# Dilated attention by pairs of heads: alternating row halves and banks for the scores, column halves for the weighing, one bias addition and one maximum per pair

## Chip, cores and metric

One core of a Trainium2 chip runs the kernel, written in Bass: every engine has its own program and waits on semaphores. The metric is device microseconds of one execution.

## What is computed

Two transformer blocks on one sequence of 256 tokens with 1024 channels, in float32: a first block with a recurrent branch, windowed attention and 32 experts, then two layers of feed-forward, mixer, feed-forward. The change is in the mixer of the last layer, dilated attention with 16 heads of 64 channels and three dilation groups. Cut to what matters:

```
qkv = (h @ w_qkv).reshape(B, T, N_GROUPS, 3, N_HEADS_2, HEAD_DIM)
for g, (window, dilation) in enumerate(DILATION_GROUPS):      # (128,1) (512,4) (2048,16)
    q = rmsnorm_2(qkv[:, :, g, 0], q_gain[g]) * (HEAD_DIM ** -0.5)
    k = rmsnorm_2(qkv[:, :, g, 1], k_gain[g])
    v = qkv[:, :, g, 2]
    logits = q k + bias, masked;  m = max;  p = exp(logits - m);  s = sum(p);  o = p v / s
    lse = m + log(s)
wts = softmax(stack(lses), axis=0)
o = sum over g of wts[g] * o[g];  return o @ w_out
```

The kernel does the three groups of a head as one softmax over their keys side by side, which is the same weighted sum.

## The kernel before

**Dense layers.** The weights come by DMA in float32 and are split into two parts whose sum is the weight: ScalarE (ACT) makes the high part (`hi_tile`, L317), VectorE (DVE) the low part (`lo_tile`, L321), TensorE (PE) multiplies with both. Layer `qkv` (72 tiles of 128 tokens by 256 columns) takes 8 chunks a tile, each one 512-column and one 256-column product (L379, L380). ACT and DVE then each take half of the result (L413, L420). Four tiles of split weights exist at a time.

**Turns.** The 16 heads are worked in four turns of four heads, each with 18 tiles of `qkv`: six with values, twelve with queries and keys. Those twelve are also squared (L1930), summed (L2109), rooted (L1918, the Sqrt table of ACT), normalised (L2104), turned on PE (L2016) and taken back (L1926). The attention of a turn is put between the chunks of the next turn's tiles. The last turn stands in the first three tiles of layer `attn_out` (L371, L372), whose chunks 6 and 7 need the last two output pairs.

**A unit of attention** is a head x and a query block b, eight units to a turn. Block 0 sees 128 keys in each group, block 1 sees 256. Its steps are: scores on PE (three products of 64 rows, L2027) into bank 3 and, for block 1, half of bank 4; on DVE the addition of the bias (L2121) and the negated maximum (L2124); Exp with its sum on ACT (L1936); on DVE reciprocal and scaling into EN (L2129, L2131); 3 or 6 transposes on PE (L2037) into bank 5, for block 1 also 6; the copy into ETX on ACT (L1945); the weighing on PE (3 or 6 products with 64 output rows, L2051) into bank 7, row half x % 2. When a pair of heads is done, ACT and DVE split its output (`out_high` L1957, `out_low` L2145), on which `attn_out` waits.

**Order.** Everything is in order of its engine's program. `STEP_BEFORE` puts ten steps 6 chunks apart from tile 4 on; step i holds the scores of unit i, the transposes of unit i-1 and the weighing of unit i-2. On ACT and DVE the steps of a turn stand among the work on a tile (`ahead`, `between`, `behind` of `run_layer`), so a step there cannot begin before the tile in front of it is out of PE. In float32 every product is two records of PE; a transpose is one.

## Time and profile before

| | |
|---|---|
| median of three runs | 2504.03 us (2503.38 to 2504.77) |
| the profiled execution, its time / its span | 2507.36 us / 2505.5 us |
| PE busy / DVE busy / ACT busy | 2397.6 us (96%) / 1404.2 us (56%) / 1010.7 us (40%) |
| `qkv` and its attention, up to the end of the last weighing | about 1960 us to 2291 us of the span |

Shares are of the whole span. The stretch of the change is about an eighth of it, and there DVE and ACT are much busier than on average, so it has to be read by windows. A PE row's duration includes its way through the array: how long PE is held is read from the distance of starts.

### The profile page before, as it was taken

How to read it: one execution, taken by the hardware profiler on the slowest of the kernel's cores; microseconds unless marked ns; L12 is line 12 of the kernel's file. 1: busy time of each engine (PE TensorE's matmuls, PEld its weight loads, DVE VectorE, ACT ScalarE, POOL GpSimd, SP SyncE). 2: the span in 40 equal slices, each digit the busy share in tenths (PEclk: the TensorE clock that was granted, in tenths of full speed). 3: DMA queues.
4: the chain of work that ended last, by engine and by line, in shares of the span. 5: the costliest groups of instructions: out<-in, count | busy, mean ns of one | idle time of the engine just before them, and what ended most of it. 6: DMA issues, size and time to landing. Idle time of an engine off the chain costs nothing.

```text
span 2505.5 us, 35586 instructions
## 1 busy us (share of the span) xinstructions
PE 2397.6 (96%) x13302; PEld 1655.2 (66%) x13303; DVE 1404.2 (56%) x2712; ACT 1010.7 (40%) x1858; POOL 75.7 (3%) x125
## 2 busy tenths in 40 slices
PE   6999999999999999999989999999999999998999
PEld 3777854444444444444468888888888778876888
DVE  5688742223222223222267779786786677776785
ACT  3645531111111111111155556654654566664653
POOL 0000000000000000000000000000000110001000
PEclk8999999999999999999999999999999999999999
DMA  8764679999999999999965555555555665552553
GB/s 311 246 230 141 215 322 424 425 426 425 425 425 425 426 426 425 426 426 425 424 223 185 180 178 182 186 184 187 183 182 193 178 137 137 141 137 71 172 181 122
DMA packets 277971, 673.68 MB, mean 269 GB/s; under 512 B 8484, under 2 KB 236111, under 8 KB 244960
## 3 DMA queue, kind: packets, MB, share of 16 engines
q1 hardware_dynamic: 274656, 663.60, 69.8%
q0 software_dynamic: 3200, 8.53, 2.5%
q8 instruction: 75, 1.23, 0.2%
q14 instruction: 40, 0.33, 0.0%
HBM read 670.45 MB, written 1.12 MB: 268 GB/s over the span
## 4 chain that ended last, share of the span: by engine, by line
PE 86%; DVE 7%; ACT 3%; DMA 2%; issue 2%; DVEq 0%; ACTq 0%; SPq 0%
PE PS L371 25%; PE PS L1454 17%; PE PS L372 13%; PE PS L1476 9%; PE PS L379 6%; PE PS L1441 5%; PE PS L380 3%; PE PS L1428 2%; DVE WS L321 2%; DMA RING<-in_moe_w 1%; PE PS L2027 1%; PE PS L2051 1%; DVE XG L1571 1%; DMA RAW<-in_w_ada 1%; PE PS L2037 1%
## 5 line engine op out<-in xcount | busy, mean ns | idle before, releaser
L371 PE MATMUL PS<-HN,WS 128*128 128x512 f32 x1952 | 704.1, 404 | 16.2 <-DVE WS L321 10.3
L321 DVE TENSOR_TENSOR WS<-RAW,WS 128x1024 fp32r<-128x1024 f32 (+1 forms) x452 | 541.0, 1205 | 136.9 <-ACT WS L317 131.3
L372 PE MATMUL PS<-HN,WS 128*128 128x256 f32 x1952 | 551.0, 282 | 0.0
L317 ACT ACTIVATE WS<-RAW 128x1024 fp32r<-128x1024 f32 (+1 forms) x452 | 463.2, 1034 | 85.8 <-PE PS L372 71.5
L1454 PE MATMUL PS<-RING,XG 128*64 128x512 f32 x2048 | 447.0, 594 | 12.0 <-DVE XG L1571 10.9
L371 PEld LDWEIGHTS PS<-HN,WS 128*128 128x128 f32 x1952 | 370.9, 190 | 111.3 <-DVE WS L321 12.5
L372 PEld LDWEIGHTS PS<-HN,WS 128*128 128x128 f32 x1952 | 373.0, 191 | 0.3
L1454 PEld LDWEIGHTS PS<-RING,XG 128*64 128x64 f32 x2048 | 148.8, 137 | 295.9 <-issue 292.3
L1577 DVE TENSOR_SCALAR GLU<-PS 128x256 f32<-128x256 f32 x64 | 27.2, 425 | 414.9 <-PE PS L1454 414.9
L371 PE MATMUL PS<-MI,WS 128*128 128x512 f32 x704 | 247.7, 397 | 0.0
L1476 PE MATMUL PS<-RING,AT 128*64 128x512 f32 x1024 | 226.8, 594 | 14.8 <-ACT AT L1350 14.8
L1343 ACT ACTIVATE SIG<-GLU 128x256 f32<-128x256 f32 x64 | 26.7, 417 | 520.6 <-DVE GLU L1577 520.6
L379 PE MATMUL PS<-WS,HN 128*128 128x512 f32 x576 | 215.1, 412 | 6.2 <-DVE WS L321 3.2
L372 PE MATMUL PS<-MI,WS 128*128 128x256 f32 x704 | 197.6, 281 | 0.0
L1476 PEld LDWEIGHTS PS<-RING,AT 128*64 128x64 f32 x1024 | 84.6, 137 | 136.4 <-issue 135.2
L380 PE MATMUL PS<-WS,HN 128*128 128x256 f32 x576 | 162.9, 283 | 0.0
L371 PEld LDWEIGHTS PS<-MI,WS 128*128 128x128 f32 x704 | 132.1, 188 | 32.0
L1571 DVE TENSOR_TENSOR XG<-PS,SH 128x512 f32<-128x512 f32 x32 | 22.1, 692 | 201.3 <-PE PS L1441 201.3
L1441 PEld LDWEIGHTS PS<-PSEL,H2K 128*128 128x128 f32 x1024 | 116.7, 192 | 25.9 <-issue 25.2
L372 PEld LDWEIGHTS PS<-MI,WS 128*128 128x128 f32 x704 | 133.0, 189 | 0.0
L379 PEld LDWEIGHTS PS<-WS,HN 128*128 128x128 f32 x576 | 109.5, 190 | 34.2 <-issue 4.1
L1441 PE MATMUL PS<-PSEL,H2K 128*128 128x64 f32 x1024 | 121.1, 276 | 0.3 <-DVE PGAT L1566 0.3
(356 smaller groups left out, 2635.4 us busy)
## 6 DMA issues: line engine op xcount, KB each, us to landing
RING<-in_moe_w SPq DMA_DIRECT2D x192, 2048.0 KB, 22.4
RAW<-in_ffn_w_in SPq DMA_DIRECT2D x88, 1024.0 KB, 5.2
...
```

Of the source, the lines that this page charges most:

```text
L317: act_f(split_tile(0, n), raw_tile(n), ACT.Copy).then_inc(hi_done, 1)
L321: vec.tensor_tensor(split_tile(1, n), raw_tile(n), split_tile(0, n).bitcast(f32), ALU.subtract).then_inc(lo_done, 1)
L371: nc.tensor.matmul(both, hi[:, k, :], x2[:, :, kx, :], start=start, stop=False)
L372: ins = nc.tensor.matmul(half, lo[:, k, :], x2[:, 0, kx, :], start=False, stop=stop)
L379: nc.tensor.matmul(both, x2[:, 0, kx, x], w2, start=start, stop=False)
L380: ins = nc.tensor.matmul(half, x2[:, 1, kx, x], w2[:, 0], start=False, stop=stop)
L1428: nc.tensor.matmul(bank[COMB[m]][:, :], PGT[64 * g:64 * g + 64, tt * P:(tt + 1) * P], YE[64 * g:64 * g + 64, :], start=True, stop=True).th ...
L1441: last = nc.tensor.matmul(bank[4][:, k * SLOTS:(k + 1) * SLOTS], H2K[:, tt, k * P:(k + 1) * P], PSEL[:, tt, :], start=tt == 0, stop=tt == ...
L1454: last = nc.tensor.matmul(bank[j][64 * side:64 * side + 64, :], XG[:, 2 * q + k, :], w[:, k, 1024 * side + 512 * j:1024 * side + 512 * (j ...
L1476: last = nc.tensor.matmul(bank[6][64 * side:64 * side + 64, :], AT[:, b, 64 * q:64 * q + 64], w[:, b, 512 * side:512 * (side + 1)], start= ...
L1571: TTN(XG[:, :, :], bank[4][:, :].rearrange("p (k s) -> p k s", k=DC), SH2[:, :].rearrange("p (k a) -> p k a", a=1).to_broadcast([P, DC, SL ...
L1577: TS(GLU[:, halves[j]], pairs[:, halves[j], 0], 7.0, None, ALU.min).then_inc(sem("clamped"), 1)
```

## The change

Two heads (x = 0 and 1, a pair p) are now one unit q, four to a turn; odd q are block 1.

- **Scores** (`scores`): head 0 uses rows 0 to 63 and bank 3, head 1 rows 64 to 127 and bank 4, one product of each in turn. For block 1 only two groups fit the banks; the third is a step of its own (`late_scores`), which waits until DVE has added the bias to the first two.
- **Weighing** (`weigh`): the products of the two heads alternate, writing partitions 0 to 63 and 64 to 127 of bank 7.
- **Bias and maximum** (`bias`): one addition over both heads and one maximum for two heads; for block 1 the addition is in two parts, 2x512 and 2x256 columns.
- **Exp, scaling, transposes, copy** remain one of each per head. For block 1 both heads' transposes use banks 5 and 6, so the odd head's wait until ACT has copied the even head's.
- **Places**: tables of offsets in chunks, units 12 chunks apart from chunk 28 on (tile 3, chunk 4). The last turn has a list for each engine.
- ES holds both heads, UB is one tensor, and the loads of a pair's bias wait for the pair.

```
-        ES = [rg(f"ES{i}", [N_GROUPS * S]) for i in range(2)]
+        ES = [rg("ES0", [2, N_GROUPS * S])]
...
+        ES.append(Region(rg.o)("ES1", [2, N_GROUPS * S]))
         DX = rg("DXT", [DC, S])
-        UB = [Region(ub0 + i * 3 * KB)(f"UB{i}", [N_GROUPS, S]) for i in range(4)]
+        UB = Region(ub0)("UB", [TURN, N_GROUPS, S])
...
-        STEP_BEFORE = {(4 + 6 * i // DC, 6 * i % DC): i for i in range(NU + 2)}
-        STEPS_AT = {w: [i for (v, k), i in STEP_BEFORE.items() if v == w + 1] for w in range(3, 10)}
-        LAST_BEFORE = {(1, 0): 0, (1, 3): 1, (2, 0): 2, (2, 3): 3}
-        OUT_AT = {11: 1}
...
-        def score_bank(n):
-            return PS[:, 3 * 512:3 * 512 + N_GROUPS * n]
-
-        def turn_bank(n):
-            return PS[:, 5 * 512:5 * 512 + N_GROUPS * n]
+        UNITS, ROUNDS = TURN, 3 * TURN // 2
+        BEGIN, APART = 28, 12
+        PE_STEPS = {"scores": 0, "late_scores": 5, "turn_even": 14, "turn_odd": 17, "weigh": 22}
+        DVE_STEPS = {"scale_even": 10, "scale_odd": 12, "bias": 0, "late_bias": 5, "out_low": 25}
+        ACT_STEPS = {"exp": 8, "take_even": 15, "take_odd": 18, "out_high": 24}
+        LAST_BEFORE = {(1, 1): [("scores", 0)], (1, 4): [("scores", 1)], (2, 1): [("late_scores", 1)], (2, 4): [("scores", 2)]}
+        LAST_PE = [("turn_even", 0), ("turn_odd", 0), ("scores", 3), ("weigh", 0), ("turn_even", 1), ("turn_odd", 1),
+                   ("late_scores", 3), ("weigh", 1), ("turn_even", 2), ("turn_odd", 2), ("weigh", 2),
+                   ("turn_even", 3), ("turn_odd", 3), ("weigh", 3)]
+        LAST_DVE = [("bias", 0), ("bias", 1), ("late_bias", 1), ("scale_even", 0), ("scale_odd", 0), ("bias", 2),
+                    ("scale_even", 1), ("scale_odd", 1), ("bias", 3), ("late_bias", 3), ("out_low", 1),
+                    ("scale_even", 2), ("scale_odd", 2), ("scale_even", 3), ("scale_odd", 3), ("out_low", 3)]
+        LAST_ACT = [("exp", 0), ("exp", 1), ("take_even", 0), ("take_odd", 0), ("exp", 2), ("take_even", 1), ("take_odd", 1),
+                    ("out_high", 1), ("exp", 3), ("take_even", 2), ("take_odd", 2), ("take_even", 3), ("take_odd", 3),
+                    ("out_high", 3)]
...
+        def rounds(U):
+            return U // 2 * 3 + U % 2
+
+        def score_banks(n):
+            return PS[:, 3 * 512:5 * 512].rearrange("p (x n) -> p x n", x=2)[:, :, 0:n]
+
+        def turn_bank(b, x):
+            at = (5 + x) * 512 if b == 0 else 5 * 512
+            return PS[:, at:at + N_GROUPS * (b + 1) * P]
...
+            def exp(c, q):
+                U, n = c * UNITS + q, N_GROUPS * (q % 2 + 1) * P
                 act.wait_ge(sem("b_max"), U + 1)
-                act_f(ES[b][:, 0:n], ES[b][:, 0:n], ACT.Exp, bias=STAT[:, 0, b:b + 1],
-                      accum_out=STAT[:, 1, b:b + 1]).then_inc(sem("b_exp"), 1)
-
-            def take_weights(c, u):
-                U, b = c * NU + u, u % 2
-                n = (b + 1) * P
-                act.wait_ge(sem("b_T"), U + 1)
-                if U >= 2:
-                    act.wait_ge(sem("b_pv"), U - 1)
-                act_f(ETX[b][:, 0:N_GROUPS * n], turn_bank(n), ACT.Copy).then_inc(sem("b_ET"), 1)
...
+            def take_weights(c, q, x):
+                U, b = c * UNITS + q, q % 2
+                act.wait_ge(sem("b_T"), 2 * U + x + 1)
+                if U:
+                    act.wait_ge(sem("b_pv"), U)
+                act_f(ETX[x][:, 0:N_GROUPS * (b + 1) * P], turn_bank(b, x), ACT.Copy).then_inc(sem("b_ET"), 1)
...
+            def scores(c, q, late=False):
+                U, p, b = c * UNITS + q, q // 2, q % 2
                 n = (b + 1) * P
-                h = slice(64 * (x % 2), 64 * (x % 2) + 64)
+                groups = (2,) if late else (0, 1) if b else (0, 1, 2)
                 pe.wait_ge(sem("q_taken"), 12 * (c + 1))
+                if rounds(U) + late:
+                    pe.wait_ge(sem("b_biased"), rounds(U) + late)
+                for i, g in enumerate(groups):
+                    for x in range(2):
+                        h = slice(64 * x, 64 * x + 64)
+                        last = nc.tensor.matmul(bank[3 + x][:, i * n:(i + 1) * n], QK[h, c % 2, 2 * g, p, b * P:(b + 1) * P],
+                                                QK[h, c % 2, 2 * g + 1, p, S - n:S], start=True, stop=True)
+                last.then_inc(sem("b_scores"), 1)
+
+            def turn_keys(c, q, x):
+                U, b = c * UNITS + q, q % 2
+                pe.wait_ge(sem("b_scaled"), 2 * U + x + 1)
                 if U:
-                    pe.wait_ge(sem("b_biased"), U)
-                for g in range(N_GROUPS):
-                    last = nc.tensor.matmul(score_bank(n)[:, g * n:(g + 1) * n], QK[h, c % 2, 2 * g, x // 2, b * P:(b + 1) * P],
-                                            QK[h, c % 2, 2 * g + 1, x // 2, S - n:S], start=True, stop=True)
-                last.then_inc(sem("b_scores"), 1)
-
-            def turn_keys(c, u):
-                U, b = c * NU + u, u % 2
-                pe.wait_ge(sem("b_scaled"), U + 1)
-                if U:
-                    pe.wait_ge(sem("b_ET"), U)
+                    pe.wait_ge(sem("b_ET"), 2 * U)
+                if b and x:
+                    pe.wait_ge(sem("b_ET"), 2 * U + 1)
                 for j in range(N_GROUPS * (b + 1)):
-                    last = nc.tensor.transpose(turn_bank(S)[:, j * P:(j + 1) * P],
-                                               EN[b][:, j * P:(j + 1) * P], IDENT)
+                    last = nc.tensor.transpose(turn_bank(b, x)[:, j * P:(j + 1) * P],
+                                               EN[x][:, j * P:(j + 1) * P], IDENT)
                 last.then_inc(sem("b_T"), 1)
...
+            def weigh(c, q):
+                U, p, b = c * UNITS + q, q // 2, q % 2
+                nk, m = b + 1, U // 2
+                pe.wait_ge(sem("b_ET"), 2 * U + 2)
                 pe.wait_ge(evacuated, qkv.t0 + c * TURN_TILES + TURN_V)
...
                 for j in range(N_GROUPS * nk):
                     g, kb = j // nk, j % nk
-                    last = nc.tensor.matmul(bank[7][h, b * P:(b + 1) * P], VV[:, c % 2, 2 * g + kb, x * HD:(x + 1) * HD],
-                                            ETX[b][:, j * P:(j + 1) * P], start=j == 0, stop=j == N_GROUPS * nk - 1)
+                    for x in range(2):
+                        v = (2 * p + x) * HD
+                        last = nc.tensor.matmul(bank[7][64 * x:64 * x + 64, b * P:(b + 1) * P], VV[:, c % 2, 2 * g + kb, v:v + HD],
+                                                ETX[x][:, j * P:(j + 1) * P], start=j == 0, stop=j == N_GROUPS * nk - 1)
                 last.then_inc(sem("b_pv"), 1)
...
-                if 0 <= c < TURNS - 1 and at in STEP_BEFORE:
-                    step(c, STEP_BEFORE[at])
+                c, w = turn_and_tile(t)
+                if 0 <= c < TURNS - 1:
+                    for kind, q in PE_AT.get((w, k), ()):
+                        step(c, kind, q)
...
-                    for i in range(len(LAST_BEFORE), NU + 2):
-                        step(TURNS - 1, i)
+                    for kind, q in LAST_PE:
+                        step(TURNS - 1, kind, q)
...
+            def bias(c, q, late=False):
+                U, p, b = c * UNITS + q, q // 2, q % 2
                 n = (b + 1) * P
-                e = ES[b][:, 0:N_GROUPS * n]
-                dve.wait_ge(sem("b_scores"), U + 1)
-                if U >= 2:
-                    dve.wait_ge(sem("b_T"), U - 1)
+                groups = slice(2, 3) if late else slice(0, 2) if b else slice(0, 3)
+                width = (groups.stop - groups.start) * n
+                e = ES[U % 2]
+                dve.wait_ge(sem("b_scores"), rounds(U) + late + 1)
+                if U >= 2 and not late:
+                    dve.wait_ge(sem("b_scaled"), 2 * U - 2)
                 if b == 0:
-                    dve.wait_ge(sem(f"ub_loaded{x}"), c * 48 + 48)
-                TTN(e.rearrange("p (g n) -> p g n", g=N_GROUPS), score_bank(n).rearrange("p (g n) -> p g n", g=N_GROUPS),
-                    UB[x][:, :, 0:n], ALU.add).then_inc(sem("b_biased"), 1)
-                dve.wait_ge(sem("b_biased"), U + 1)
-                vec.tensor_reduce(STAT[:, 0, b:b + 1], e, AX.X, ALU.max, negate=True).then_inc(sem("b_max"), 1)
...
-            def invert(c, u):
-                b = u % 2
-                dve.wait_ge(sem("b_exp"), c * NU + u + 1)
-                o.link(vec.reciprocal(STAT[:, 4, b:b + 1], STAT[:, 1, b:b + 1]))
-                ordered, e = (t[b][:, 0:N_GROUPS * (b + 1) * P].rearrange("p (g n) -> p g n", g=N_GROUPS) for t in (EN, ES))
-                TS(ordered, e[:, :, ::-1], STAT[:, 4, b:b + 1], None, ALU.mult).then_inc(sem("b_scaled"), 1)
-
...
+                TTN(e[:, :, groups.start * n:groups.stop * n].rearrange("p x (g n) -> p x g n", n=n),
+                    score_banks(width).rearrange("p x (g n) -> p x g n", n=n),
+                    UB[:, 2 * p:2 * p + 2, groups, 0:n], ALU.add).then_inc(sem("b_biased"), 1)
+                if b == 0 or late:
+                    dve.wait_ge(sem("b_biased"), rounds(U) + late + 1)
+                    vec.tensor_reduce(STAT[:, U % 2, :], e[:, :, 0:N_GROUPS * n], AX.X, ALU.max, negate=True).then_inc(sem("b_max"), 1)
+
+            def invert(c, q, x):
+                U, b = c * UNITS + q, q % 2
+                dve.wait_ge(sem("b_exp"), 2 * U + x + 1)
+                if U:
+                    dve.wait_ge(sem("b_T"), 2 * U + x - 1)
+                r = STAT[:, 4 + U % 2, x:x + 1]
+                o.link(vec.reciprocal(r, STAT[:, 2 + U % 2, x:x + 1]))
+                n = N_GROUPS * (b + 1) * P
+                ordered, e = (t.rearrange("p (g n) -> p g n", g=N_GROUPS) for t in (EN[x][:, 0:n], ES[U % 2][:, x, 0:n]))
+                TS(ordered, e[:, :, ::-1], r, None, ALU.mult).then_inc(sem("b_scaled"), 1)
...
-            for i in range(NU + 2):
-                step(TURNS - 1, i)
-                scale(TURNS - 1, i)
-            out_low(DC - 1)
+            for kind, q in LAST_DVE:
+                step(TURNS - 1, kind, q)
```

PE in the last turn, behind chunk 5 of tile 2, before. EN_183 and EN_184 are the scaled weights of the two blocks, ETX_181 and ETX_182 their turned copies; SM is the identity.

```order
6633 L2027 MATMUL PS<-QK 128x128 [waits b_biased,q_taken]
6634 L2027 MATMUL PS<-QK 128x128 x2
6635 L2037 MATMUL PS<-SM,EN_184 128x128 [waits b_ET,b_scaled]
6636 L2037 MATMUL PS<-SM,EN_184 128x128 x5
6637 L2051 MATMUL PS<-ETX_181,VV 64x128 [waits ox_lo,evacuated,b_ET]
6638 L2051 MATMUL PS<-ETX_181,VV 64x128 x2
6639 L2027 MATMUL PS<-QK 128x256 [waits b_biased,q_taken]
6640 L2027 MATMUL PS<-QK 128x256 x2
```

And of the change, where EN_182 and EN_183, ETX_180 and ETX_181 belong to the two heads:

```order
6671 L2065 MATMUL PS<-SM,EN_182 128x128 [waits b_ET,b_scaled]
6672 L2065 MATMUL PS<-SM,EN_182 128x128 x2
6673 L2065 MATMUL PS<-SM,EN_183 128x128 [waits b_ET,b_scaled]
6674 L2065 MATMUL PS<-SM,EN_183 128x128 x2
6675 L2053 MATMUL PS<-QK 128x256 [waits b_biased,q_taken]
6676 L2053 MATMUL PS<-QK 128x256 x3
6677 L2080 MATMUL PS<-ETX_180,VV 64x128 [waits ox_lo,evacuated,b_ET]
6678 L2080 MATMUL PS<-ETX_181,VV 64x128
6679 L2080 MATMUL PS<-ETX_180,VV 64x128
6680 L2080 MATMUL PS<-ETX_181,VV 64x128
```

Where one head's products stood in a row, the two heads now alternate, and transposes of both heads of a unit come together.

DVE in a turn between tiles 4 and 5 of `qkv`, before (the tile's half is the row of L420):

```order
1458 L420 SCALAR_TENSOR_TENSOR VV<-PS,RSC,VV 128x256 [waits half_out]
1459 L2121 TENSOR_TENSOR ES_180<-PS,UB_188 128x768 [waits b_T,b_scores]
1460 L2124 TENSOR_REDUCE STAT<-ES_180 128x1 [waits b_biased]
1461 L321 TENSOR_TENSOR WS<-RAW_66,WS 128x1024 [waits hi_done]
1462 L2129 RECIPROCAL STAT<-STAT 128x1 [waits b_exp]
1463 L2131 TENSOR_SCALAR EN_184<-ES_180,STAT 128x768 [waits dve_own]
1464 L321 TENSOR_TENSOR WS<-RAW_66,WS 128x1024 [waits hi_done]
```

And of the change, from the half of tile 5 on:

```order
1455 L420 SCALAR_TENSOR_TENSOR VV<-PS,RSC,VV 128x256 [waits half_out]
1456 L2167 RECIPROCAL STAT<-STAT 128x1 [waits b_T,b_exp]
1457 L2170 TENSOR_SCALAR EN_182<-ES_185,STAT 128x768 [waits dve_own]
1458 L321 TENSOR_TENSOR WS<-RAW_66,WS 128x1024 [waits hi_done]
1459 L2154 TENSOR_TENSOR ES_179<-PS,UB 128x2x384 [waits ub_loaded2,ub_loaded3,b_scaled,b_scores]
1460 L2159 TENSOR_REDUCE STAT<-ES_179 128x2 [waits b_biased]
1461 L2167 RECIPROCAL STAT<-STAT 128x1 [waits b_T,b_exp]
1462 L2170 TENSOR_SCALAR EN_183<-ES_185,STAT 128x768 [waits dve_own]
```

The odd head's scaling of unit 1 (1461, 1462) now stands behind a weight split, and behind addition and maximum of unit 2.

ACT in a turn, around the work on tile 8, of the change; the order of kinds is that of before, but the Exp of two heads stand where one stood:

```order
1070 L413 ACTIVATE QRAW_170<-PS,RSC 128x256 [waits mm_done,q_normed]
1071 L1957 ACTIVATE QSQ_173<-QRAW_169 128x256 [waits evacuated]
1072 L1945 ACT_TABLE_LOAD
1073 L1945 ACTIVATE QST<-QST,EPSC 128x4 [waits q_summed]
1074 L1964 ACT_TABLE_LOAD
1075 L1964 ACTIVATE ES_185,STAT<-ES_185,STAT 128x768 [waits b_max]
1076 L1964 ACTIVATE ES_185,STAT<-ES_185,STAT 128x768
1077 L1972 ACTIVATE ETX_180<-PS 128x768 [waits b_pv,b_T]
```

Both Exp of unit 3 stand behind the tile's half, a square, a table load, a root and a second table load.

## Rows read from the trace of the kernel before

**Rows 1.** The page: busy time of each engine, share of the span
```profile
PE 2397.6 (96%) x13302; PEld 1655.2 (66%) x13303; DVE 1404.2 (56%) x2712; ACT 1010.7 (40%) x1858; POOL 75.7 (3%) x125
```
**Rows 2.** Windows: stretch of attention, rest of a turn, the last turn
```profile
core 0: us, PE busy (x) PEld busy (x) DVE busy (x) ACT busy (x) POOL busy (x), PEclk, DMA share, GB/s
2015.49:2062.38 46.89, 44.62 (x268) 35.31 (x267) 34.25 (x55) 28.95 (x50) 6.38 (x12) 1.00 0.63 121
2062.38:2096.85 34.47, 34.45 (x202) 29.87 (x202) 25.06 (x51) 23.25 (x52) 0.00 (x0) 1.00 0.49 158
...
2256.25:2291.27 35.02, 28.76 (x182) 22.18 (x181) 19.95 (x33) 12.28 (x26) 0.00 (x0) 1.00 0.01 1
```
**Rows 3.** Chain that ended last: start, us, what; two steps of a turn
```profile
2028.55 1.49 PE PS L2027 x6
...
2030.52 1.45 PE PS L2051 x12
...
2034.28 0.86 PE PS L2027 x6
2035.14 0.80 PE PS L2037 x6
2035.95 0.80 PE PS L2051 x6
```
**Rows 4.** Timeline of PE: chunks around the end of a step
```profile
2026.17 0.50 PE L379 MATMUL PS<-WS,HN 128*128 128x512 f32 x1
...
2026.62 0.40 PE L379 MATMUL PS<-WS,HN 128*128 128x512 f32 x1
...
2028.04 0.40 PE L379 MATMUL PS<-WS,HN 128*128 128x512 f32 x1
...
2028.48 1.56 PE L2027 MATMUL PS<-QK 64*128 64x256 f32 x6
```
**Rows 5.** Groups by form, PE, 340 to 420 us, the experts
```profile
L1454 PE MATMUL PS<-RING,XG 128*64 128x512 f32 x192 | 41.9, 594 | 1.0 <-DVE XG L1571 1.0
```
**Rows 6.** Timeline of PE: the experts' combination and what follows
```profile
707.41 1.99 PE L1428 MATMUL PS<-YE,PGT 64*128 64x512 f32 x8
709.33 0.44 PE L1462 MATMUL PS<-SM,PGAT 128*128 128x128 f32 x2
```
**Rows 7.** Groups by form, 1960 to 2310 us: DVE's and ACT's attention
```profile
L2121 DVE TENSOR_TENSOR ES<-PS,UB 128x768 f32<-128x768 f32 x16 | 15.3, 957 | 13.2 <-PE PS L2027 13.2
L2124 DVE TENSOR_REDUCE STAT<-ES 128x1 f32<-128x768 f32 x16 | 15.2, 953 | 0.6
...
L2121 DVE TENSOR_TENSOR ES<-PS,UB 128x384 f32<-128x384 f32 x16 | 8.8, 548 | 4.0 <-PE PS L2027 4.0
```
**Rows 8.** Timeline of ACT and DVE behind a query tile
```profile
2049.67 0.46 ACT L413 ACTIVATE QRAW<-PS,RSC 128x256 f32<-128x256 f32 x1
...
2050.03 0.41 ACT L1930 ACTIVATE QSQ<-QRAW 128x256 f32<-128x256 f32 x1
2050.46 1.28 ACT L1918 ACT_TABLE_LOAD   x1
...
2051.75 0.30 ACT L1918 ACTIVATE QST<-QST,EPSC 128x4 f32<-128x4 f32 x1
2052.07 1.28 ACT L1936 ACT_TABLE_LOAD   x1
...
2054.61 0.94 ACT L1936 ACTIVATE ES<-ES,STAT 128x768 f32<-128x768 f32 x1 [1.26 <-DVE STAT L2124]
...
2055.67 0.16 DVE L2129 RECIPROCAL STAT<-STAT 128x1 f32<-128x1 f32 x1 [1.09 <-ACT ES L1936]
2055.87 1.01 DVE L2131 TENSOR_SCALAR EN<-ES,STAT 128x768 f32<-128x768 f32 x1
```
**Rows 9.** Groups by form, 1960 to 2310 us: the weight splits
```profile
L321 DVE TENSOR_TENSOR WS<-RAW,WS 128x1024 fp32r<-128x1024 f32 x78 | 93.3, 1221 | 7.4 <-ACT WS L317 5.3
L317 ACT ACTIVATE WS<-RAW 128x1024 fp32r<-128x1024 f32 x77 | 78.4, 1047 | 0.0
```

134 lines of the change are left out of this document (62 added, 72 removed).

## The prediction, made before the run
> **What bounds the kernel now.** I read the page first: PE is busy 96% of the span [rows 1]. Then the windows of the stretch that the change touches. In a turn's stretch of attention, of which there are three alike, PE is busy 44.62 of 46.89 us, so 2.27 us are waits; in the rest of a turn it has none (34.45 of 34.47). In the last turn it is busy 28.76 of 35.02 us, waits 6.26 [rows 2]. DVE has 34.25 us of work in the 46.89, 73%, far above its 56% on the page [rows 1, 2]. So PE's own time sets the end here, with DVE close enough that it must be watched, and what is taken from PE is worth its full time until DVE or ACT is late.
>
> PE's own time is read from starts, not durations. A block-1 unit holds PE 1.49 us with scores and 1.45 us with weighing, a block-0 unit 0.86 and 0.80 [rows 3]. Two heads: 2 x (1.49 + 1.45 + 0.86 + 0.80) = 9.2 us; eight pairs make 73.6 us. A score record is held 1.49/6 = 0.248 us at 256 columns and 0.86/6 = 0.143 at 128, that is 0.82 ns a column and some 0.04 us on top; a weighing record 1.45/12 = 0.121 us or 0.80/6 = 0.133.
>
> **Term 1, alternation on PE.** No row before has alternating halves at 128 or 256 columns. The nearest are at 512. In the experts, L1454 writes the two column halves in turn: 192 records take 41.9 us, 0.218 each [rows 5]. By the line through 128 and 256 columns a record of 512 that runs alone would take 0.143 + 384 x 0.82 ns = 0.458 us, so two halves run at once there and even the extra 0.04 is gone. L1428 alternates row halves: eight records from 707.41 to 709.33, 0.24 each [rows 6]. I model it so: of a product's two records the second runs together with the first of the other half, so m products take m + 1 records' time. (L1428 has m = 4: 5 x 0.458 = 2.3, it took 1.92, so this is on the careful side.) Per pair, with the single record's full time, extra included: scores of block 0, m = 6, 7 x 0.143 = 1.0; block 1 early, m = 4, 5 x 0.248 = 1.24; late, m = 2, 3 x 0.248 = 0.74; weighing block 0, 7 x 0.133 = 0.93; block 1, m = 12, 13 x 0.121 = 1.57. Sum 5.5. Perfect halving would give 4.6, and a little less with the extra hidden. I take 5.0, between the ends and on neither: a pair saves 4.2 us, a turn 8.4. The bounds of the saving: 3.7 to 4.6 if it works, nothing if at this size it doesn't (then 9.2 stays).
>
> The Trainium skill ("TensorE: Matmul & The Clock Gate", Part 3, What overlaps and what doesn't) says that a weight load overlaps running products only when its row group differs; two column halves share all rows, so by that rule the weighing would gain little and the pair only some 2.2 us, 17 us less over eight pairs. [Rows 5] speak against it at 512 columns, and the measurement decides.
>
> **Term 2, insertions.** Leaving and re-entering the dense stream costs: from 2026.17 to 2028.48 stand six chunks, 2.31 us, while four chunks take 1.42 (0.355 each) [rows 4]; 2.31 - 2.13 = 0.18 us, about 0.09 for each of two changes. Before there are ten places with scores or weighing in a turn, after also ten (four scores, two late scores, four weighings). The transposes use the whole array like the dense products. I cost it at nothing, with at most 0.5 us a turn.
>
> **Term 3, DVE.** Addition: (957 - 548)/384 = 1.065 ns a column [rows 7]. A pair had 2 x 0.548 + 2 x 0.957 = 3.01 us; now 768 columns 0.96, 1024 columns 1.23, 512 columns 0.68, together 2.87. The maximum of 768 is 0.953 [rows 7]; with the same slope 1536 columns take 1.77. Before 4 maxima, by that slope 3.0 us; after 2.7. DVE loses 0.4 us of work a pair, nothing on PE's path. The loads of the bias come in two bursts of six instead of four of three; they are needed a turn later, so cost nothing. ACT's work is unchanged.
>
> **Term 4, new waits.** Without any, the stretch from chunk 28 to the last weighing would need PE 44.62 + 4 chunks (1.41) - 8.4 = 37.6 us, against 48.3 (46.89 + 1.41) before. But DVE has about 33.4 us of work in it, plus tile 3's. So I walked through a turn along the three programs, with distances from [rows 3, 4, 7 to 9]. Four places are late, all where a step on ACT or DVE stands behind a tile's work:
>
> - Unit 3, even head's transposes. Exp stands behind tile 8's half (0.36), square (0.43), table load, root and second load (from 2050.46 to 2053.35: 2.9), so 3.7 us after PE finishes tile 8 it may begin; then 0.1 to start, 1.06 to the reciprocal, 0.2, scaling 1.0, 0.06: 6.1 [rows 8]. PE arrives after six chunks and the weighing of unit 2, 2.1 + 1.0 = 3.1. It waits 3.0 us.
> - Unit 1, odd head's transposes. From the end of tile 5: half 0.5, weight split on ACT 1.0, Exp 1.0, then DVE alone: reciprocal and scaling 1.2, split 1.15, addition and maximum of unit 2 1.9, reciprocal and scaling 1.2, start-up 0.1 [rows 7 to 9]: 8.0. PE arrives after nine chunks 3.2, weighing 0.9, scores 1.0, six transposes 0.8, changes 0.2: 6.1. It waits 1.9.
> - Weighing of unit 3: ACT's copy stands behind tile 9's half, square, load, root and a split, 4.1 us after that tile with its own 0.7; PE arrives at 3.5. 0.6.
> - Units 0 and 1, begin of the turn: Exp behind two splits and a load (0.4); late scores behind the early addition (0.4).
>
> Together 6.3 us. A turn's stretch then takes 37.6 + 6.3 = 43.9, saves 48.3 - 43.9 = 4.4; three turns 13.2. The 2.27 of waits before are inside these figures. The bounds of Term 4: nothing late (then 10.7 a turn), or 9 us of waits (1.7 a turn).
>
> **Term 5, the last turn.** PE needs 28.76 - 8.4 = 20.4. Waits, by the same walk: the first scaling stands behind the late addition and the 1.77 of unit 1's maximum (0.5); the late scores of unit 1 behind the early addition (0.3); the pair of transposes of unit 1, where the odd head waits for scaling, then for ACT's copy out of the shared banks (0.5 + 0.8); scores 3 behind addition 2 (0.5); transposes 2 behind the second long maximum and its Exp-free path on DVE (2.0); unit 3's shared banks again (0.8), and its last copy (0.8), weighing and odd remainders 0.5. Sum 6.7. So 27.1 against 35.02: 7.9 saved.
>
> **Sum.** 13.2 + 7.9 = 21.1 us. The profiled execution took 2507.4 us (span 2505.5), 3.3 us above the median of the runs, 2504.0; taken from the median: 2483 us.
>
> **Rivals.**
>
> *Full gain* (0.12). The waits of Term 4 don't come, since ACT and DVE run ahead more than I walked. For it: before, with steps as densely placed, only 2.27 us were lost. Against: the chain behind tile 8 is made of rows alone. Then 3 x 10.7 + 7.9 = 40: 2464 us.
>
> *Alternation gives nothing at this size* (0.12). The extra 0.04 us of a record could be its weight load, which at 128 columns is over a quarter of it; if loads of two halves can't run together with products, a pair stays at about 9.2. PE is then slower than the chains of Term 4, so some 1 us of wait is left: 48.3 - (46.0 + 1.0) = 1.3 a turn and 1 in the last, 5 us: 2499 us, at the edge of no change. Against: the 0.218 of [rows 5].
>
> *Only the scores gain* (0.08). 2.2 us a pair instead of 4.2, 4.4 a turn, waits down to about 4: 48.3 - (46.0 - 4.4 + 4.0) = 2.7 a turn and 4 in the last: 2492 us. This is what the skill's rule above would make; [rows 5] speak against it.
>
> *Slower* (0.05). Each change of half drains the array, as a change between dense and attention products does, at 0.09 us [rows 4]. A pair has 30 products, so 30 changes: 2.7 us on top of 9.2, with no overlap. Eight pairs lose 21.6, the placing gives back 5: 2504 + 17 = 2521 us. It decides from 0.02 us a change on. [Rows 5, 6], where halves change every second record at 0.218 and 0.24 us, speak against it.
>
> The forecast has 0.63. Its own range, with 3 to 9 us of waits a turn and 3.7 to 4.6 saved a pair, is 2473 to 2492. For eight times in ten I reach towards both neighbours: 2466 to 2497. A difference under 0.2%, 5 us, is what a measurement of this kernel can't tell from none. Faster by more than that: forecast, full gain, scores alone, and half of "nothing": 0.89. Same 0.06, slower 0.05.
>
> **What would show it.** In the new trace, the starts of a block-1 weighing should span about 1.5 us for 24 records and of block-0 scores about 0.9 for 12; the stretch from a turn's first scores to its last weighing should take some 44 us, with PE waiting for DVE's scaling before the transposes of unit 3 (3 us) and the odd ones of unit 1 (2 us); the last turn some 27 us from its first scores. The prediction is wrong if a weighing record still takes 0.12 us, if the waits before transposes are under 2 us or over 10 us a turn, or if time comes back in `attn_out`, whose chunks wait for the last output pair as before.

## The result, and the profile after

The change takes 2490.98 us (median of six runs, 2486.87 to 2496.72), the kernel before 2504.4 in the same comparison: a ratio of 0.9941, 95% interval 0.9924 to 0.9958. It is faster, by 13.4 us, and inside the range of the prediction, but 8 us behind its 2483. The profiled execution took 2494.54 us, 12.8 less than that of before.

The page of the change, busy time of each engine:

```profile
PE 2372.0 (95%) x13302; PEld 1634.2 (66%) x13303; DVE 1398.6 (56%) x2688; ACT 1011.6 (41%) x1858; POOL 76.0 (3%) x125
```

PE has 25.6 us less work than in [rows 1], and only half of that has reached the span. The windows tell where the rest is. First turn's stretch, rest of that turn, second and third stretch, last turn (first scores to the end of the last weighing):

```profile
2015.60:2062.28 46.68, 40.97 (x275) 32.84 (x275) 32.70 (x49) 29.39 (x50) 6.34 (x12) 0.89 0.53 124
2062.28:2095.17 32.89, 32.89 (x196) 28.81 (x194) 25.45 (x52) 23.14 (x52) 0.00 (x0) 1.00 0.50 161
2095.17:2139.99 44.82, 38.09 (x275) 30.27 (x274) 32.40 (x49) 29.39 (x50) 6.34 (x12) 0.96 0.54 129
2172.91:2217.43 44.52, 38.27 (x275) 30.38 (x274) 32.40 (x49) 29.39 (x50) 6.34 (x12) 0.96 0.55 130
2249.23:2278.48 29.25, 22.21 (x179) 16.18 (x178) 18.64 (x27) 11.75 (x25) 0.00 (x0) 0.92 0.00 1
```

Against 48.3 before (46.89 and the four chunks 28 to 31), the three turns gain 1.6, 3.5 and 3.8 us, and the last 5.8 of its 35.02 [rows 2]: 14.7, where 21.1 was forecast. Three turns do the same work with the same 275 records, yet PE is busy 40.97, 38.09 and 38.27 us. The last column but two tells why: the granted clock was 0.89, 0.96 and 0.96, and 0.92 in the last turn, while before it was 1.00 in the same four stretches.

The products themselves, in the chain of the change (start, us, what). The second column is how long the records held PE:

```profile
2015.68 0.87 PE PS L2053 x12
...
2025.34 0.70 PE PS L2053 x4
...
2039.56 1.46 PE PS L2080 x24
...
2041.91 1.06 PE PS L2053 x8
```

And a weighing of block 0 in PE's timeline, with the chunk behind it:

```profile
2048.05 0.88 PE L2080 MATMUL PS<-ETX,VV 128*64 128x128 f32 x12
2048.85 0.50 PE L379 MATMUL PS<-WS,HN 128*128 128x512 f32 x1
```

A pair's products are: scores of block 0 12 records in 0.87, early scores of block 1 8 in 1.06, late ones 4 in 0.63 to 0.70, weighing of block 1 24 in 1.46; weighing of block 0 takes 0.80 for 12, from start to start. Sum 4.8 to 4.9 against 9.2 in [rows 3]. One head's 0.86, 1.45 and 0.80 is now what two heads take.

The waits, in the timeline of PE. The bracket is the idle time ahead of the row and who ended it:

```profile
2035.36 1.31 PE L2065 MATMUL PS<-SM,EN 128*128 128x128 f32 x6 [1.91 <-DVE EN L2170]
...
2053.53 1.54 PE L2065 MATMUL PS<-SM,EN 128*128 128x128 f32 x6 [3.01 <-DVE EN L2170]
...
2114.93 0.88 PE L2065 MATMUL PS<-SM,EN 128*128 128x128 f32 x6 [1.91 <-DVE EN L2170]
```

Both forecast waits are there, at 1.91 and 3.01 us for 1.9 and 3.0. But behind them the same six transposes take 1.31 and 1.54 us in the first turn and 0.88 in the second, behind the same wait. Windows of 5 us around the two places in the first turn:

```profile
2030.00:2035.00 5.00, 3.45 (x28) 2.83 (x28) 4.89 (x7) 3.06 (x5) 0.24 (x1) 1.00 0.82 116
2035.00:2040.00 5.00, 4.64 (x26) 4.01 (x28) 2.61 (x5) 2.00 (x5) 0.00 (x0) 0.66 0.49 161
2040.00:2045.00 5.00, 5.00 (x45) 3.92 (x41) 2.44 (x5) 2.76 (x6) 0.00 (x0) 1.00 0.17 54
...
2050.00:2055.00 5.00, 1.99 (x11) 1.66 (x10) 3.65 (x9) 3.14 (x5) 0.71 (x2) 0.77 0.95 145
2055.00:2060.00 5.00, 5.00 (x21) 4.48 (x20) 1.60 (x5) 4.33 (x7) 0.00 (x0) 0.55 0.63 192
```

Late in a wait or shortly after it (0.85 in 2052 to 2053, 0.82 in 2035 to 2036) the clock falls to the lower of its two levels, 1.2 of 2.4 GHz, for some microseconds: in the last window PE is busy all the time, and gets 21 records done at 0.55. The last turn has such stretches too; its first scores, 12 records, held PE 1.54 us instead of 0.87. That can't be put down to the new waits: it stands behind two waits for turned queries just ahead of the turn, 1.79 and 2.19 us, and before has the same two, 1.80 and 2.17 us, with a low clock behind them that is over when its first scores begin, at 2256.25. A window of before:

```profile
2252.00:2256.00 4.00, 3.30 (x12) 2.88 (x12) 1.12 (x5) 1.62 (x4) 0.00 (x0) 0.59 0.75 250
```

### The profile page after: what moved, and what is told of

Read it like the earlier page. It is cut to its first block, busy times and chain, and to the rows that moved or that the text cites. A ratio compares the mean times of both kernels' runs of the same rounds, so it can differ in the third digit from the quotient of the medians.

```text
span 2492.7 us, 35558 instructions
## 1 busy us (share of the span) xinstructions
PE 2372.0 (95%) x13302; PEld 1634.2 (66%) x13303; DVE 1398.6 (56%) x2688; ACT 1011.6 (41%) x1858; POOL 76.0 (3%) x125
## 3 DMA queue, kind: packets, MB, share of 16 engines
q8 instruction: 75, 1.23, 0.2%
## 4 chain that ended last, share of the span: by engine, by line
PE 83%; DVE 7%; ACT 4%; issue 3%; DMA 2%; DVEq 0%; ACTq 0%; SPq 0%
PE PS L371 25%; PE PS L1454 17%; PE PS L372 13%; PE PS L1476 9%; PE PS L379 5%; PE PS L1441 5%; PE PS L1428 2%; PE PS L380 2%; DVE WS L321 2%; DMA RING<-in_moe_w 1%; DVE XG L1571 1%; ACT WS L317 1%; PE PS L759 1%; DMA RAW<-in_w_ada 1%; PE PS L2065 1%
## 5 line engine op out<-in xcount | busy, mean ns | idle before, releaser
L1577 DVE TENSOR_SCALAR GLU<-PS 128x256 f32<-128x256 f32 x64 | 27.2, 425 | 415.0 <-PE PS L1454 415.0
L1476 PE MATMUL PS<-RING,AT 128*64 128x512 f32 x1024 | 226.8, 594 | 14.8 <-ACT AT L1350 14.8
L379 PE MATMUL PS<-WS,HN 128*128 128x512 f32 x576 | 222.3, 422 | 6.2 <-DVE WS L321 3.2
```

What stands on the lines that cost most here:

```text
L379: nc.tensor.matmul(both, x2[:, 0, kx, x], w2, start=start, stop=False)
L1476: last = nc.tensor.matmul(bank[6][64 * side:64 * side + 64, :], AT[:, b, 64 * q:64 * q + 64], w[:, b, 512 * side:512 * (side + 1)], start= ...
L1577: TS(GLU[:, halves[j]], pairs[:, halves[j], 0], 7.0, None, ALU.min).then_inc(sem("clamped"), 1)
```

## The experiments

Eleven kernels, each the change with one edit, or with two or three of them together. The theory after the trace: the products gain fully, the waits are those of the walk, and what is missing is the clock behind the waits. The rivals: the gain of the products is smaller than the rows suggest, DVE's merged operations cost something on the path, or the waits have other causes than the order on ACT and DVE. Stretches of the profiled executions, in us with the granted clock, each from the first scores to the end of the last weighing; the turns of the change are repeated for comparison. The column "whole" runs from the first scores of turn 1 to the last weighing of the last turn, 277.2 us before, from the place of chunk 28 on:

| | turn 1 | turn 2 | turn 3 | last | whole | median, ratio to before (95%) |
|---|---|---|---|---|---|---|
| change | 46.7 (0.89) | 44.8 (0.96) | 44.5 (0.96) | 29.3 (0.92) | 262.9 | 2490.98, 0.9941 (0.9924 to 0.9958) |
| scores_in_rows | 43.9 (1.00) | 44.7 (0.96) | 44.3 (0.96) | 31.2 (0.83) | 261.4 | 2485.1, 0.9923 (0.99 to 0.9946) |
| weigh_in_rows | 46.7 (0.96) | 45.4 (1.00) | 45.4 (1.00) | 31.1 (0.94) | 265.7 | 2492.55, 0.9943 (0.9925 to 0.996) |
| weigh_by_twos | 45.3 (0.96) | 46.8 (0.89) | 45.0 (0.96) | 29.8 (0.90) | 263.7 | 2488.88, 0.9952 (0.9933 to 0.9971) |
| max_per_head | 46.7 (0.89) | 44.9 (0.96) | 44.6 (0.96) | 30.0 (0.90) | 263.9 | 2489.96, 0.9951 (0.9938 to 0.9965) |
| fill_waits | 43.6 (1.00) | 43.6 (1.00) | 43.6 (1.00) | 27.2 (1.00) | 255.1 | 2485.29, 0.9921 (0.9905 to 0.9938) |
| odd_scale_earlier | 42.7 (0.96) | 43.2 (0.96) | 43.8 (0.92) | 30.6 (0.83) | 257.6 | 2481.99, 0.9907 (0.9891 to 0.9924) |
| odd_scale_and_fill | 42.2 (1.00) | 42.2 (1.00) | 42.2 (1.00) | 27.4 (0.99) | 251.6 | 2479.14, 0.9902 (0.9886 to 0.9919) |
| exp_earlier | 50.5 (0.90) | 49.0 (0.93) | 49.0 (0.93) | 27.3 (1.00) | 273.0 | 2499.37, 0.9968 (0.9954 to 0.9982) |
| scale_earlier | 43.6 (0.96) | 44.7 (0.96) | 46.2 (0.89) | 30.8 (0.83) | 262.6 | 2486.97, 0.9918 (0.9893 to 0.9942) |
| exp_and_scale_earlier | 41.7 (0.96) | 40.4 (1.00) | 41.7 (0.96) | 27.2 (1.00) | 248.1 | 2476.0, 0.9895 (0.9877 to 0.9912) |
| late_scores_later | 40.7 (1.00) | 40.7 (1.00) | 40.7 (1.00) | 31.3 (0.83) | 250.9 | 2476.49, 0.9881 (0.9857 to 0.9905) |

What lies ahead of the first turn is the same program in these twelve kernels, yet it took 2006.9 to 2019.9 us in their profiled executions. That is a spread of 13 us where nothing was edited, larger than most effects of the edits. So the medians, with 4 to 10 runs each, tell only the large differences, and the stretches are what an edit is read by.

### What the alternation is worth

scores_in_rows gives each head's products of a scores step in a row, still two heads in one step:

```
-                for i, g in enumerate(groups):
-                    for x in range(2):
+                for x in range(2):
+                    for i, g in enumerate(groups):
```

> The changed kernel with the score products of a unit in rows again: all of head 0, then all of head 1; banks, places and everything else stay. If alternation is what pays, twelve 128-column records go from 0.87 us back to 2 x 0.86, eight 256-column ones from 1.06 to about 2.0, four from 0.63 to 1.0: 2.1 us a pair, 17 us over eight. The wait before the odd transposes of unit 1 hides 0.85 us of it in each turn, so 13 to 15 us come back and the ratio to before is about 1.000. If the gain came from the new places and the shared addition, the ratio stays at 0.994.

weigh_in_rows does the same with the weighing:

```
-                for j in range(N_GROUPS * nk):
-                    for x in range(2):
+                for x in range(2):
+                    for j in range(N_GROUPS * nk):
```

> The changed kernel with the weighing products of a unit in rows: all of head 0, then all of head 1. If alternation of column halves pays, twelve records go from 0.8 to 1.6 us and twenty-four from 1.46 to 2.9: 2.2 us a pair. Two waits for DVE in a turn hide 0.8 us each, so 10 to 12 us come back, ratio about 0.999. If weight loads of two column halves can't overlap, as the skill has it, nothing comes back: ratio 0.994, and the records take the same time in rows.

The chain of scores_in_rows:

```profile
2006.99 1.19 PE PS L2053 x12
...
2029.63 1.46 PE PS L2080 x24
2031.98 1.07 PE PS L2053 x8
2035.33 0.63 PE PS L2053 x4
```

And of weigh_in_rows:

```profile
2019.97 0.87 PE PS L2053 x12
...
2042.28 2.38 PE PS L2080 x24
2045.57 1.06 PE PS L2053 x8
2048.92 0.63 PE PS L2053 x4
```

Neither went as expected: in rows the products are not serial. Twelve records of scores take 1.19 us, where two heads apart took 2 x 0.86 = 1.72 [rows 3]: 0.53 saved, at 0.143 a record 3.7 records. Eight of 256 columns take 1.07 where four of each alone would be 8 x 0.248 = 1.98: 0.91, again 3.7 records, and no more than alternation saves. Twenty-four of the weighing take 2.38 for 2.90: 0.52, at 0.121 4.3 records. So PE runs about four records of the next half beside the last four of this one. With four records to a head or fewer, order is free; above that alternation adds 0.3 us (scores, and weighing of block 0, 1.08 for 0.80) and 0.9 (weighing, block 1). For the scores that is 0.32 x 8 = 2.6 us in all, and such a kernel doesn't come out slower than the change: the intervals overlap, and its first turn, at a clock of 1.00, is 2.8 us shorter. For the weighing it is 1.2 x 8 = 9.6 us of PE's work; the two turns of weigh_in_rows at 1.00 take 45.4 us, 1.8 more than a turn at 1.00 with alternation (43.6, fill_waits below), since some of it falls into waits. In the medians, 0.9943 for 0.9941, where 10 to 12 us were expected, nothing of it can be told.

weigh_by_twos tests the reading with blocks of four records:

```
-                for j in range(N_GROUPS * nk):
-                    for x in range(2):
+                js = range(N_GROUPS * nk)
+                twos = [(j, x) for a in js[::2] for x in range(2) for j in js[a:a + 2]]
+                for j, x in twos:
```

> Only the order of the weighing's products changes: two products of one head (four records), then two of the other, and so on. In the kernels with the heads in a row about four records of the second head ran beside the first. If PE looks about four records ahead, blocks of four records overlap as fully as single products: 24 records in 1.5 to 1.6 us (1.46 in the change), 12 in 0.8 to 0.9, and the time is that of the change, 2491 us (ratio 0.994). Rival: only a record next to a change of half overlaps: a block of four gains one or two, 24 records take 1.9 to 2.2 us and 12 about 1.1, eight pairs lose 3 to 4 us: 2494 to 2495 us.

Its chain:

```profile
2032.37 1.51 PE PS L2082 x24
2034.78 1.06 PE PS L2053 x8
```

1.51 us against 1.46: blocks of four overlap as well as single products, within 0.05. The look-ahead reading stands, its rival (only a record next to a change overlaps, 1.9 to 2.2) falls. By what mechanism PE does it, these runs don't show.

### The clock

fill_waits puts idle products, whose results nobody reads, where PE waits: eight in each of three turns, work that is added and leaves the output as it is.

```
+                if c < TURNS - 1:
+                    for _ in range({(3, 0): 5, (1, 1): 3}.get((q, x), 0)):
+                        nc.tensor.matmul(bank[7][:, S:2 * S], IDENT, SM[:, 0:2 * P], start=True, stop=True)
```

> The changed kernel with idle-time products that nobody reads: in each of the first three turns five 256-column float32 products of constants ahead of the even transposes of unit 3 (2.5 us into a wait of 3.0) and three ahead of the odd transposes of unit 1 (1.5 us into 1.9), into an unused half of bank 7. They lengthen PE's work and shorten no chain. If the fall of the granted clock behind these waits (0.89, 0.96, 0.96 over the three stretches) is what the prediction lacked, the clock stays at 1.00 there and the stretches shrink from 46.8, 44.9 and 44.5 us to about 44: 3 to 6 us less than the change, ratio 0.992. If only the waits themselves cost, nothing changes: 0.994.

Windows of fill_waits: first stretch, rest of the turn, last turn.

```profile
2010.37:2053.95 43.58, 40.10 (x291) 31.81 (x291) 32.42 (x49) 29.36 (x50) 6.37 (x12) 1.00 0.57 133
2053.95:2086.85 32.90, 32.90 (x196) 28.78 (x194) 25.75 (x52) 23.14 (x52) 0.00 (x0) 1.00 0.49 161
2238.25:2265.46 27.21, 20.20 (x179) 14.54 (x178) 18.63 (x27) 12.21 (x26) 0.00 (x0) 1.00 0.00 1
```

PE in front of the even transposes of unit 3, and its wait for the weighing of that unit:

```profile
2043.54 2.32 PE L2061 MATMUL PS<-SM 128*128 128x256 f32 x10
2046.72 0.87 PE L2068 MATMUL PS<-SM,EN 128*128 128x128 f32 x6 [0.86 <-DVE EN L2173]
2048.14 0.38 PE L2040 MATMUL PS<-SM,QNR 128*128 128x128 f32 x2
...
2052.49 1.53 PE L2083 MATMUL PS<-ETX,VV 128*64 128x128 f32 x24 [1.20 <-ACT ETX L1972]
```

And the two fillings of the first turn by themselves, windows of line L2061 alone:

```profile
2025.00:2029.90 4.90, 1.46 (x6) 1.06 (x6) 1.00 0.74 119
2043.00:2046.30 3.30, 2.32 (x10) 1.82 (x10) 1.00 0.90 76
```

The ten records cover 2.1 us of the 3.0, and the transposes behind them take 0.87 instead of 1.54. With more work on PE the three filled turns are shorter and all alike, 43.58 us at 1.00. The last turn has no filling in this kernel and still ran at 1.00, in 27.21 us; that is not the filling's doing, as far as this run shows. Both are near the prediction's 43.9 and 27.1.

That the filling keeps the clock up is seen over all profiled turns. Filled ones, here and in odd_scale_and_fill below, ran at 1.00 in 6 of 6; unfilled ones with a wait of 2.7 us or more in front of unit 3's even transposes (the change and seven of the kernels) in 3 of 24. Of the runs without a profile only the mean clock of the whole kernel is known: 0.984 to 0.987 in the change, 0.986 to 0.990 in fill_waits, so it may not have held in each of them. In time, fill_waits is 5 us ahead of the change by the ratios (0.9921 for 0.9941), but the intervals overlap, and scores_in_rows has 0.9923 without any filling. What the clock costs is therefore shown by the traces and not by the medians.

From the busy time the clock can be priced. The fillings took 1.46 + 2.32 = 3.8 us; each begins about 0.16 us ahead of the end of the row in front of it, so they add 3.5, and a turn's own work at 1.00 is 40.10 - 3.5 = 36.6 us. Two unfilled turns at 1.00 agree: the first of scores_in_rows is busy 37.29, less 2 x 0.32 for its order 36.65, the second of weigh_in_rows 39.03, less 2 x 1.2 again 36.6. The change was busy 40.97, 38.09 and 38.27, and 22.21 in the last turn against 20.20. The low clock cost PE 4.3, 1.5, 1.6 and 2.0: 9.4 us. The four stretches became only 7.3 us longer by it (165.3 for 158.0), because a slower PE comes later to the weighing of unit 3 and waits less there: 0, 1.0 and 0.5 us for 1.2.

odd_scale_earlier moves one step on DVE by a chunk:

```
-        DVE_STEPS = {"scale_even": 10, "scale_odd": 12,
+        DVE_STEPS = {"scale_even": 10, "scale_odd": 11,
```

> The changed kernel with the offset of the odd head's scaling at 11 instead of 12, which puts it on DVE ahead of addition and maximum of unit 2, not behind them. If the wait of 1.9 us before the odd transposes of unit 1 is made by these two (0.95 each), it goes; the three turns lose 1.9 us each and turn 1, whose clock falls behind this wait, some 2 more: 6 to 8 us less than the change, ratio 0.991. If DVE is the bound of the stretch, the same time comes back at the scores of unit 3 or the transposes of unit 2: ratio 0.994.

The wait of 1.9 before the odd transposes of unit 1 is gone in all three turns: it did come from a scaling behind a weight split and unit 2's bias. The late scores wait 0.7 for 0.3. The ratio is 0.9907 for the change's 0.9941, some 8 us, though the intervals touch; in the trace the whole is 5.3 us shorter, about the three waits of 1.9.

odd_scale_and_fill has both:

```
-        DVE_STEPS = {"scale_even": 10, "scale_odd": 12,
+        DVE_STEPS = {"scale_even": 10, "scale_odd": 11,
...
+                filled = {(3, 0): 5} if c < TURNS - 1 else {(2, 0): 2, (1, 1): 1, (3, 1): 1}
+                if c == TURNS - 1 and (q, x) == (2, 0):
+                    pe.wait_ge(sem("ox_lo"), U // 2)
+                for _ in range(filled.get((q, x), 0)):
+                    nc.tensor.matmul(bank[7][:, S:2 * S], IDENT, SM[:, 0:2 * P], start=True, stop=True)
```

> The odd scaling one chunk earlier (its wait of 1.9 us a turn went in the run that had it alone) and idle products, whose results nobody reads, put where PE otherwise waits: five in front of unit 3's even transposes in three turns, four in the last turn. It adds work that leaves the output as it is. If the lower granted clock after waits is what kept the gain below the forecast, the clock stays at 1.00 in all turns, a turn takes 42 to 42.5 us (43.6 with filling alone, less the 1.9, plus 0.4 for the late scores), the last 27.2, and the time is 2478 to 2481 us (0.990). Rival: the two gains don't add, since a shorter turn moves the wait to the next late step (late scores, weighing of unit 3), and it ends at 2482 to 2485 us, as each of the two alone.

Turns of 42.2 at 1.00, the last 27.4, 2479.14 us, all as expected. The interval is nearly that of odd_scale_earlier, so in the medians the two gains are not told apart from one; in the traces they add, 1.4 us a turn below fill_waits and 6.0 us in the whole below odd_scale_earlier. Here the mean clock of every run fits: 0.989 to 0.990 in all four, 0.986 to 0.987 in the four of odd_scale_earlier.

### Where the wait of 3 us comes from

Exp of unit 3 stands on ACT behind tile 8's half, a square, a root and two table loads; its scaling on DVE stands behind the same tile's normalising. Three kernels move the one, the other and both.

```
-        DVE_STEPS = {"scale_even": 10, "scale_odd": 12,
+        DVE_STEPS = {"scale_even": 7, "scale_odd": 9,
...
-        ACT_STEPS = {"exp": 8,
+        ACT_STEPS = {"exp": 7,
```

scale_earlier has the first of these edits, exp_earlier the second, exp_and_scale_earlier both.

> Both Exp of a unit are one chunk earlier (in front of tile 8's half, with the Exp table still loaded, so that a table load falls away), and both scalings three chunks earlier on DVE, the even one in front of tile 8's work. If the 3.0 us of wait before unit 3's even transposes come from that order on ACT alone, they go, no other wait of more than 1 us takes their place, and the engine's granted clock stays higher behind them: turns of about 42 us instead of 44.5 to 46.7, and about 2480 to 2483 us (ratio 0.990 to 0.9915). Rival: the two Exp now stand in front of the tile's half, PE gets its bank later, and what the transposes gain is given back there: 2490 us, turns as in the change. Odd transposes of unit 1 (wait 1.9) should lose their wait too, since their scaling is earlier in the program.

> Only the Exp of each unit is one chunk earlier on ACT; the scalings stay where the change has them. In the run with both moved, the root of tile 8 came 0.30 us at 2048.82, and DVE could normalise from 2049.15 on. Here DVE's scaling still stands behind that normalising, so it starts at about 5.2 us behind the weighing of unit 2, and the even transposes of unit 3 at about 6.4, against 5.5 in the change: the wait stays at 3 to 4 us and the time at 2489 to 2493 us (ratio 0.994 to 0.9955). Rival: it was ACT's order alone (two table loads in front of Exp), then the wait goes and the time is 2480 to 2484 us.

> Only the scalings are three chunks earlier on DVE; Exp stays behind tile 8's half, the root and two table loads. The even scaling of unit 3 can't start before Exp ends (wait of 3.0 us stays), and DVE now waits for it in front of tile 8's half, so the turned queries of that tile come later and PE may wait there too. The odd transposes of unit 1 lose their 1.9 us, the late scores of unit 1 gain up to 1.8. Net: 2486 to 2492 us (0.993 to 0.995). Rival: the places of the scalings were the whole matter, then it is 2476 to 2480 us, as with both moved.

ACT, DVE and PE in exp_earlier, first turn, unit 3 and tile 8:

```profile
2051.58 0.94 ACT L1964 ACTIVATE ES<-ES,STAT 128x768 f32<-128x768 f32 x1 [2.17 <-DVE STAT L2159]
...
2055.51 0.30 ACT L1945 ACTIVATE QST<-QST,EPSC 128x4 f32<-128x4 f32 x1
...
2056.05 0.43 DVE L2134 TENSOR_TENSOR QNR<-QRAW,QST 128x256 f32<-128x256 f32 x1
...
2056.59 1.01 DVE L2170 TENSOR_SCALAR EN<-ES,STAT 128x768 f32<-128x768 f32 x1
...
2057.65 1.54 PE L2065 MATMUL PS<-SM,EN 128*128 128x128 f32 x6 [4.60 <-DVE EN L2170]
```

In scale_earlier:

```profile
2046.33 0.94 ACT L1964 ACTIVATE ES<-ES,STAT 128x768 f32<-128x768 f32 x1
...
2047.39 0.16 DVE L2167 RECIPROCAL STAT<-STAT 128x1 f32<-128x1 f32 x1 [2.74 <-ACT ES L1964]
...
2048.66 0.88 PE L2065 MATMUL PS<-SM,EN 128*128 128x128 f32 x6 [3.02 <-DVE EN L2170]
```

And in exp_and_scale_earlier:

```profile
2044.89 0.94 ACT L1964 ACTIVATE ES<-ES,STAT 128x768 f32<-128x768 f32 x1 [1.56 <-DVE STAT L2159]
...
2046.15 1.01 DVE L2170 TENSOR_SCALAR EN<-ES,STAT 128x768 f32<-128x768 f32 x1
...
2047.22 0.87 PE L2065 MATMUL PS<-SM,EN 128*128 128x128 f32 x6 [0.24 <-DVE EN L2170]
...
2049.84 0.44 PE L2040 MATMUL PS<-SM,QNR 128*128 128x128 f32 x2 [1.05 <-DVE QNR L2134]
```

With Exp alone, weights are ready at 2052.5 and lie four microseconds until DVE has normalised the tile, which itself waits for a root that Exp has pushed back: the wait is 4.60 us instead of 3.01, two more of 2.3 and 2.2 come in each turn (which I had not foreseen), the whole is 10 us longer than in the change, and the ratio rises from 0.9941 to 0.9968, though the intervals just overlap. With scaling alone the wait stays, 3.02, as expected; the odd one of unit 1 goes, and one of 1.9 before the late scores takes its place. The whole is 262.6 for 262.9, so nothing is gained, and the 6 us of the ratio (0.9918, intervals overlapping) can't be put down to the edit. With both, the wait of 3 us is 0.24, and a new one of 1.05 appears for the turned queries. Each order holds the other fast. This is the largest step found: the whole is 14.8 us shorter than in the change, and 2476.0 us is below the change and before with intervals apart.

In exp_and_scale_earlier the late scores of unit 1 wait 1.78 us, since the early addition comes behind scaling. late_scores_later puts them five chunks later on PE:

```
-            for x, kind, q in sorted((BEGIN + APART * q + o, kind, q) for kind, o in offsets.items()
+            for x, kind, q in sorted((BEGIN + APART * q + o + (5 if kind == "late_scores" and q == 1 else 0), kind, q)
+                                     for kind, o in offsets.items()
```

> Both moves of exp_and_scale_earlier, and besides the late scores of unit 1 stand five chunks later on PE, so that dense chunks fill the 1.78 us that it waited there for the early addition; DVE's order is as it was. If DVE's chain behind them has slack, a turn gets 1.8 us shorter, waits 1.6 instead of 3.4, clock 1.00 throughout: turns of 39 to 40 us instead of 40.4 to 41.7, and 2469 to 2473 us (0.987 to 0.988). Rival: the addition, the long maximum, Exp and scaling behind the late scores have no slack, and the wait comes again before the transposes of unit 1: 2476 us, no difference from the run without this edit.

PE in it, unit 1, first turn:

```profile
2029.73 0.87 PE L2066 MATMUL PS<-SM,EN 128*128 128x128 f32 x6 [1.42 <-DVE EN L2171]
2032.44 0.84 PE L2066 MATMUL PS<-SM,EN 128*128 128x128 f32 x6 [0.79 <-ACT ETX L1973]
```

The rival was right: the wait moved to the transposes of unit 1, 1.42 and 0.79 for 1.78. A turn at 1.00 takes 40.7 us for 40.4, so the edit gains nothing. The three turns are together 1.8 us shorter, because none of them had a low clock; the last one ran at 0.83 and is 4.0 longer, and the ratio, 0.9881, can't be told from 0.9895.

### One maximum per pair

```
-                    vec.tensor_reduce(STAT[:, U % 2, :], e[:, :, 0:N_GROUPS * n], AX.X, ALU.max, negate=True)
+                    vec.tensor_reduce(STAT[:, U % 2, 0:1], e[:, 0, 0:N_GROUPS * n], AX.X, ALU.max, negate=True)
+                    vec.tensor_reduce(STAT[:, U % 2, 1:2], e[:, 1, 0:N_GROUPS * n], AX.X, ALU.max, negate=True)
```

> Undoes one part of the change: the maximum is taken per head (two operations for a unit) instead of one per pair. By the rows 2 x 0.95 instead of 1.75 us at 768 columns a head and 2 x 0.55 instead of 0.95 at 384, so DVE has 0.15 us more in each unit. If the merged maximum was off PE's path the time is that of the change within 1 us: 2491 us (0.994). Rival: DVE is on the path in front of the odd scaling of unit 1, in front of the late scores and in the last turn, so that 0.15 to 0.3 come four or five times a turn, and the lower clock after longer waits doubles it: 2494 to 2496 us.

Groups by form of max_per_head on DVE, 1990 to 2310 us:

```profile
L2159 DVE TENSOR_REDUCE STAT<-ES 128x1 f32<-128x768 f32 x8 | 7.6, 954 | 0.3
L2160 DVE TENSOR_REDUCE STAT<-ES 128x1 f32<-128x768 f32 x8 | 7.5, 943 | 0.0
```

Two take 1.90 us where the merged one takes 1.75, and the turns are as in the change (46.7, 44.9, 44.6). This part of the change is worth nothing that can be measured.

## Why the prediction was right, and where its size was off

**What bounds the kernel**: right. PE's own time set the end, and DVE and ACT became late only at single places.

**Term 1**, 5.0 us a pair, 4.2 saved: measured 4.8 to 4.9, so 4.3 to 4.4 saved. The model of m + 1 records was too careful throughout: 1.46, not 1.57, and 0.80, not 0.93, for the weighing; 0.87, not 1.0, 1.06, not 1.24, and 0.63 to 0.70, not 0.74, for the scores. At 128 columns m products take the time of m records that run alone. The Trainium skill ("TensorE: Matmul & The Clock Gate", Part 3, What overlaps and what doesn't) lets a weight load overlap only if the row group differs; the weighing's halves are halves of columns, and 24 records took 1.46 us for 2.90, so here the measurement decides against it. The reason that the prediction gave, alternation, was only partly the reason: two heads in one step already overlap about four records.

**Term 2**, nothing for insertions: nothing in the traces speaks against it. Own work of a turn came to 36.6 us, 1.0 below the 37.6 of Term 4's first line; 0.2 to 0.4 of that is Term 1, the rest I can't assign.

**Term 3**, DVE: additions 0.96, 1.22 and 0.69 for 0.96, 1.23 and 0.68; maxima 0.95 and 1.75 for 0.95 and 1.77. Off the path, as said.

**Term 4**, 6.3 us of waits a turn: the waits in the three turns sum to 5.7, 6.7 and 6.3 us, and the two large ones hit within 0.01. What failed is the step from waits to time, "37.6 + 6.3 = 43.9": it took PE's work as the same at any clock. The stretch was 46.7, 44.8 and 44.5 because 4.3, 1.5 and 1.6 us more went into the same records at the lower clock.

**Term 5**, 27.1 for the last turn: 29.25, with 6.97 of waits for the 6.7 walked; again 2.0 us of it is the clock, 0.7 of them in the first scores, behind waits that before has too.

**Sum.** 21.1 forecast, and 14.7 in the four stretches (12.8 in the span, whose part ahead of them came out longer in this execution): 9.4 us of clock were left out, and own work was 3 x 1.0 + 0.2 = 3.2 us less than priced; 21.1 - 9.4 + 3.2 = 14.9, within 0.2 of the 14.7. fill_waits, whose four stretches all ran at 1.00, gives 3 x (48.3 - 43.58) + (35.02 - 27.21) = 22.0 us. So the sum was right for a clock of 1.00, with some luck: two errors cancel in it. A turn's own work was 1.0 us less than priced, and its waits at 1.00 come to 6.9 instead of 6.3, 43.6 - 36.6, since the weighing of unit 3 waits 1.2 us and not 0.6.

**The rivals.** *Full gain*: no, since the waits came. *Nothing at this size* and *only the scores*: no, by the 1.46. That the time ended at 2491, beside the 2492 of "only the scores", is chance; its mechanism isn't in the trace. *Slower*: no.

What stays open: why the same wait of 1.91 us is followed by a low clock in the first turn and not in the second; in the last turn of before, waits of 1.81 and 2.41 us stand beside 1.00. The low stretches also differ between kernels with the same last turn: waits of 6.9 us stood beside 1.00 in fill_waits and 0.83 in odd_scale_earlier. With one trace for each kernel that can't be told from chance, and it is worth up to 4 us of a run; differences of 2 or 3 us between single kernels here should not be explained by their edits.
